# The down stage of a hybrid decoder step: prompt tokens stationary and 512 weight columns moving, the 32 sample tokens in full precision on four column groups

## The chip, the cores and the metric

The kernel runs on one core of a Trainium2 chip. Its engines are TensorE (PE; PEld in the profile is its weight load), VectorE (DVE), ScalarE (ACT), GpSimd (POOL) and SyncE (SP), which issues most DMAs. The metric is the device time of one execution in microseconds (us); lower is better.

## What is computed

One inference step of a two-layer decoder for 256 prompt tokens and 32 sample tokens (8 sequences of 4), model width 1024. The change touches the second half of the PEER channel mixer that ends each layer. There every one of 16384 experts has a row in `u_tab` and a row in `v_tab`; each token picks some experts, and

```python
act = jax.nn.gelu(jnp.einsum('td,thkd->thk', tb, u_tab[eb]))     # up
return jnp.einsum('thk,thkd->td', (gb * act), v_tab[eb])         # down
...
xp = xp + mp[5][:, None, :] * peer_ffn(...)                      # gated residual
```

The kernel computes it densely: a table W of 128 blocks x 128 experts holds for every token the gated activation (zero where the token did not pick the expert), and the down stage is the product y = W^T v over all 16384 experts: [288 tokens x 16384] times [16384 x 1024], in float32.

## The kernel before, in words

All weights come as 680 tiles of 128 x 1024 float32 words (512 KB) that SP loads in order into `ring`, a ring of four buffers; a buffer is loaded again when the PE has finished with its tile (semaphore `tile_done`). Float32 is reached with fp32r matmuls, in which each operand is split into a high part (an fp32r copy) and a low part (the rest): high x high, low x high and high x low, three passes. `wt_hi` (two buffers) is the high part of a weight tile, written by ACT (`high`, line 368, signals `hi_ready`); `ring_lo` lies on the same memory as `ring` and is the low part, written over the tile by DVE in this stage (line 2027, signals `lo_v`).

In the down stage of a layer (lines 1432 to 1456, 128 tiles for each of the two layers) tile j holds the rows of the 128 experts of block j. One tile is called a slot here. The activations `W[:, j]` (128 x 288) are split too: `w_hi` (two buffers, ACT, line 477, `wh_ready`) and `w_lo` (POOL, line 2116, `wl_ready`). For each of eight 128-column chunks c of the weight tile, the chunk is the stationary operand and the 288 tokens are the moving one; the sum of chunk c grows in PSUM bank c, with model columns on the partitions and tokens along the row. That makes 3 passes x 8 = 24 matmuls a slot (lines 1440, 1444, 1448). ACT prepares two tiles ahead: `down_high` waits for `tile_done` of slot n, then writes `w_hi` and `wt_hi` for tile n+2.

After the last slot DVE adds the sums to the residual stream `xT` with the gate (`residual`, lines 1748 to 1753, chunk by chunk out of PSUM), and the next part starts on its signal `x_ready`.

Two other places of the kernel matter for reading its trace. The V projection of the attention (lines 872 to 892) already has prompt tokens stationary and 512 weight columns moving in fp32r (`v_tile`, 884 and 892), and its 32 sample tokens in full precision on four column groups (`v_samples`, 872: four matmuls with 32 stationary columns each, whose results go to four groups of 32 partitions). The QK stage has a norm on four column groups (line 831, 288 columns) between two fp32r tiles (823 before it, 816 behind it).

Of the kernel before, what the change touches and what calls it, by code (L numbers as in the profile page):

```python
# [22 lines left out]
NC = D // P  # L23
SP_, SB, ST = 256, 8, 4
T = SP_ + SB * ST
# [22 lines left out]
UT, VT = (120, 424), (248, 552)  # L48
# [4 lines left out]
HI = (16, 52 + 256)  # L53
# [11 lines left out]
ACT = mybir.ActivationFunctionType  # L65
# [26 lines left out]
def build(nc, I, O):  # L92
    ctx = ExitStack()
    with ctx:
        def sb(name, words, dt=F32):
            return ctx.enter_context(nc.sbuf_tensor(name, [P, words], dt))

        def sem(name):
            return ctx.enter_context(nc.semaphore(name))


        big = sb("big", 128 * T)
# [16 lines left out]
        y_lo, y_hi = (split_t[:, z * NC * T:(z + 1) * NC * T].rearrange("p (c t) -> p c t", c=NC) for z in range(2))  # L119
        h_hi, h_lo = (split_t[:, z * NC * T:(z + 1) * NC * T].rearrange("p (c t) -> p c t", c=NC) for z in range(2))  # L120
        w_hi = w_hi_t[:, 0:2 * T].rearrange("p (b t) -> p b t", b=2)
        w_lo = split_t[:, 0:2 * T].rearrange("p (b t) -> p b t", b=2)
        xT_t = sb("xT", NC * T)
        xT = xT_t[:, :].rearrange("p (c t) -> p c t", c=NC)
# [2 lines left out]
        ada = ada_t[:, :].rearrange("p (l j c r) -> p l j c r", l=L, j=6, c=NC)  # L127
# [3 lines left out]
        ident = consts[:, 256:384]  # L131
# [10 lines left out]
        gtmp = sb("gtmp", 2 * T)  # L142
# [6 lines left out]
        ps = ctx.enter_context(nc.psum_tensor("ps", [P, 8, 512], F32))  # L149
# [14 lines left out]
        W = big[:, :].rearrange("p (j t) -> p j t", j=128)  # L164
# [103 lines left out]
        assert rb.at <= 128 * T - NC * T  # L268
        v_turn = gtmp[:, 0:512]
        jsum = small[:, 0:32]  # L270

        def unit_p(u):
            return (p_two if u >= H else p_one)[u % 4][:, 0:384 * (u // H + 1)]
# [31 lines left out]
        def kv_slot(n):  # L305
# [11 lines left out]
            "gelu_done w_done aq_copied aq_sq aq_ms aq_sd aq_qn aq_rot aq_done v_copied qz_ready "  # L317
            "us_mm us_half us_max us_exp us_t us_cpa us_cpv us_pv us_o ss_mm ss_max ss_exp ss_t ss_cp "
            "ss_norm ss_pv oT_ready out_done st_out kv_out glu_used_v "
            "aq_rc aq_sp hq_ready hq_lo hq_lo_v yh_ready yl_ready ss_oc ss_ot s5_rmr s5_zl hi_ready lo_u lo_v hh_ready hl_ready wh_ready wl_ready").split()}  # L320
        tile_in = [sem(f"tile_in{s}") for s in range(RING)]

        def tile_wait(eng, n, i=0):
# [41 lines left out]
        def high(act, n, i=0):  # L365

            tile_wait(act, n, i)
            nc.scalar.activation(wt_hi[:, n % 2], ring[:, n % RING], ACT.Copy).then_inc(S["hi_ready"], 1)  # L368

        def peer_act(act, l):  # L370
# [95 lines left out]
            for n in range(GROUPS):  # L466
                gate_high(n)
                if n == GROUPS - 1:
                    act.wait_ge(S["x_out"], 16 * (l + 1))
                    act.dma_start(xT_t[:, :], x_keep).then_inc(S["x_back"], 16)  # L470
                    for b in range(2):
                        nc.scalar.activation(w_hi[:, b], W[:, b], ACT.Copy).then_inc(S["wh_ready"], 1)
                gelu_split(n)


            def w_high(j, b):
                nc.scalar.activation(w_hi[:, b], W[:, bass.ds(j, 1), :].rearrange("p a t -> p (a t)"), ACT.Copy)\  # L477
                   .then_inc(S["wh_ready"], 1)

# [2 lines left out]
            def down_high(i, s):  # L482
                act.wait_ge(S["tile_done"], 4 * i + (VT[l] + s + 1))
                w_high(4 * i + (s + 2), s % 2)
                high(act, VT[l] + s + 2, i)
# [3 lines left out]
                    down_high(i, s)  # L489
            for s in range(2):  # L490
                down_high(31, s)

        def attention_act(act, root_mean):

# [589 lines left out]
        def _(pe):  # L1084
            mm = nc.tensor.matmul
# [214 lines left out]
            def peer_pe(l):  # L1300
# [87 lines left out]
                for n in range(2):  # L1388
                    for q in range(3):
                        ins = nc.tensor.transpose(ps[:, n, 128 * q:128 * q + 128],  # L1390
                                                  sel3[:, q, 8 * n:8 * n + 8, :].rearrange("p u k -> p (u k)"), ident)
                    ins.then_inc(S["sel_t"], 1)
                for q in range(3):
                    ins = mm(ps[:, 2, 32 * q:32 * q + 32], selz[:, q, :], jsel, start=True, stop=True)
# [35 lines left out]

                pe.wait_ge(S["gb_cp"], GROUPS * (l + 1))

                def down(i, first, last=False):
                    for s in range(4):
                        pe.wait_ge(S["hi_ready"], 4 * i + (HI[l] + 128 + s + 1))
                        pe.wait_ge(S["wh_ready"], 4 * i + (128 * l + s + 1))
                        for c in range(NC):
                            if first and s == 0 and c == 6:
                                pe.wait_ge(S["gelu_done"], 128 * (l + 1))
                            mm(ps[:, c, 0:T], wt_hi[:, s % 2, c * 128:(c + 1) * 128], w_hi[:, s % 2],  # L1440
                               start=(first and s == 0), stop=False, skip_group_check=True)
                        pe.wait_ge(S["wl_ready"], 4 * i + (128 * l + s + 1))
                        for c in range(NC):
                            mm(ps[:, c, 0:T], wt_hi[:, s % 2, c * 128:(c + 1) * 128], w_lo[:, s % 2],  # L1444
                               start=False, stop=False, skip_group_check=True)
                        pe.wait_ge(S["lo_v"], 4 * i + (LOV[l] + GROUPS + s + 1))
                        for c in range(NC):
                            ins = mm(ps[:, c, 0:T], ring_lo[:, s, c * 128:(c + 1) * 128], w_hi[:, s % 2],  # L1448
                                     start=False, stop=(last and s == 3), skip_group_check=True)
                        ins.then_inc(S["tile_done"], 1)  # L1450

                down(0, True)
                with pe.Fori(1, 31) as i:
                    down(i, False)
                down(31, False, True)

            peer_pe(0)
            mean_square(2)
# [119 lines left out]
        def _(v):  # L1578
            own = Count(v, S["v_own"])
            TT, TS, STT, CP = (nc.vector.tensor_tensor, nc.vector.tensor_scalar, nc.vector.scalar_tensor_tensor,  # L1580
                               nc.vector.tensor_copy)
# [8 lines left out]
            for r in range(4):  # L1590
                ins = nc.vector.memset(tmask[32 * r:32 * r + 32, 32 * r:128], 1.0)
# [97 lines left out]
            for z in range(2):  # L1689
# [183 lines left out]
            def peer_dve(l):  # L1873
                last = S["q_copied"]
                v.wait_ge(last, 8 * l + 8)
                TT(qsq, qraw, qraw, ALU.mult).then_inc(S["qsq_ready"], 1)
                for n in range(2):
# [4 lines left out]
                    ins = TT(q, q, r, ALU.mult)  # L1882
# [141 lines left out]
                with v.Fori(0, 32) as i:  # L2024
                    for s in range(4):
                        v.wait_ge(S["hi_ready"], 4 * i + (HI[l] + 128 + s + 1))
                        TT(ring_lo[:, s], ring[:, s], wt_hi[:, s % 2].bitcast(F32), ALU.subtract)\  # L2027
                            .then_inc(S["lo_v"], 1)
                v.wait_ge(S["x_back"], 16 * (l + 1))
                v.wait_ge(S["tile_done"], VT[l] + 128)  # L2030
                residual(ada[:, l, 5], ps[:, :, 0:T], 0, NC, gtmp[:, 0:256].rearrange("p (c t) -> p c t", c=NC),
                         S["x_ready"])

            modulate(1)
            ada_finish(1, 0, 6, 12)
# [261 lines left out]
```

## Time and profile before

| | |
|---|---|
| time of the kernel, median of 3 runs | 2474.07 us (2470.76 to 2480.36) |
| time of the profiled execution | 2485.71 us |
| its span, first to last instruction | 2483.9 us |
| busy: PE, DVE, ACT, POOL | 95%, 60%, 39%, 28% of the span |
| mean granted TensorE clock | 0.963 of full |
| down stage, layer 0 and layer 1 | 803.6 to 1212.3 us and 2066.7 to 2475.3 us |

The profile is one execution. Times in the rows are us from the span's start; a row of the timeline gives start, length, engine, line, operation, output<-inputs, shape and count, and in brackets the idle time before it with what ended it. A matmul that runs in full float32 shows as two records, one in fp32r as one. The two down stages together take a third of the span.

### The profile page before, as it was taken

Reading aid. Unit: us, or ns where it says so; the run is one execution under the profiler, and the core shown is the slowest. Engines: PE = TensorE matmul, PEld = TensorE weight load, DVE = VectorE, ACT = ScalarE, POOL = GpSimd, SP = SyncE. Lnnn points to the kernel's source line nnn. Section 1 sums busy time; section 2 is a strip of 40 time slices with the busy share of each in tenths; the row PEclk is TensorE's granted clock in tenths of the full one; section 3 lists DMA queues with packets and bytes.
Section 4 is the critical chain, followed back from the end, with each engine's and each line's share of the span. In section 5 each row is a group of like instructions: output and inputs, shape, how many; then the busy total and the mean of one; then the engine's idle time right before and its main releaser. Section 6 shows DMA issues by size and latency. Waiting matters only on the chain.

```text
span 2483.9 us, 50343 instructions
## 1 busy us (share of the span) xinstructions
PE 2361.9 (95%) x18518; PEld 2225.1 (90%) x18518; DVE 1478.9 (60%) x3301; ACT 979.5 (39%) x1675; POOL 705.1 (28%) x488
## 2 busy tenths in 40 slices
PE   6899999999999999999698977999999999999998
PEld 3578799999999999999697655999999999999998
DVE  8743369888898333333535442399688995333333
ACT  3234154444443444444332430443444434444443
POOL 2036267900000222222264200479300001222222
PEclk9968999999999999999899988999999999999999
DMA  8854544433334444444632662444433334444444
GB/s 311 286 181 159 203 138 165 138 136 128 127 127 144 163 165 164 166 163 168 241 127 94 257 252 98 136 161 142 143 128 129 127 127 165 167 163 166 165 165 137
DMA packets 105472, 404.98 MB, mean 163 GB/s; under 512 B 13377, under 2 KB 13633, under 8 KB 102177
## 3 DMA queue, kind: packets, MB, share of 16 engines
q1 hardware_dynamic: 99216, 360.84, 42.8%
q10 hardware_dynamic: 6160, 42.91, 4.4%
q8 instruction: 55, 0.90, 0.2%
q14 instruction: 41, 0.33, 0.0%
HBM read 394.56 MB, written 9.14 MB: 163 GB/s over the span
## 4 chain that ended last, share of the span: by engine, by line
PE 71%; issue 16%; POOL 9%; DMA 2%; DVE 2%; ACT 0%; ACTq 0%; SPq 0%; POOLq 0%; DVEq 0%
PE ps L1448 11%; PE ps L1440 11%; PE ps L1444 11%; POOL ring_lo L2098 8%; PE ps L1420 6%; PE ps L1419 6%; PE ps L1423 6%; PE ps L1407 5%; DMA ring<-in_stream 2%; PE ps L1094 2%; PE ps L1318 1%; POOL ring_lo L2105 1%; PE ps L816 1%; PE ps L820 1%; PE ps L823 1%
## 5 line engine op out<-in xcount | busy, mean ns | idle before, releaser
L368 ACT ACTIVATE wt_hi<-ring 128x1024 fp32r<-128x1024 f32 x564 | 593.9, 1053 | 344.6 <-PE ps L1318 209.5
L2027 DVE TENSOR_TENSOR ring_lo<-ring,wt_hi 128x1024 fp32r<-128x1024 f32 x256 | 314.7, 1230 | 492.1 <-ACT wt_hi L368 492.1
L2116 POOL TENSOR_TENSOR split<-big,w_hi 128x288 fp32r<-128x288 f32 x256 | 208.0, 813 | 1201.7 <-PE ps L1423 603.3
L2098 POOL TENSOR_TENSOR ring_lo<-ring,wt_hi 128x1024 fp32r<-128x1024 f32 x112 | 308.4, 2760 | 127.8 <-ACT wt_hi L368 127.8
L1419 PE MATMUL ps<-split,wt_hi 128*128 128x288 f32 x1152 | 328.5, 307 | 0.0
L1420 PE MATMUL ps<-split,wt_hi 128*128 128x288 f32 x1152 | 316.1, 298 | 0.0
L1448 PE MATMUL ps<-w_hi,ring_lo 128*128 128x288 f32 x2048 | 313.1, 295 | 1.4 <-DVE ring_lo L2027 1.4
L1444 PE MATMUL ps<-split,wt_hi 128*128 128x288 f32 x2048 | 313.1, 295 | 0.3
L1440 PE MATMUL ps<-w_hi,wt_hi 128*128 128x288 f32 x2048 | 312.9, 295 | 0.0
L477 ACT ACTIVATE w_hi<-big 128x288 fp32r (+1 forms) x252 | 112.0, 445 | 452.7 <-PE ps L1448 452.7
L1448 PEld LDWEIGHTS ps<-w_hi,ring_lo 128*128 128x128 f32 x2048 | 285.5, 188 | 1.9 <-DVE ring_lo L2027 1.9
L1444 PEld LDWEIGHTS ps<-split,wt_hi 128*128 128x128 f32 x2048 | 285.5, 188 | 0.8 <-POOL split L2116 0.8
L1440 PEld LDWEIGHTS ps<-w_hi,wt_hi 128*128 128x128 f32 x2048 | 285.5, 188 | 0.0
L1314 PE MATMUL ps<-split,wt_hi 128*128 128x288 f32 x896 | 247.4, 300 | 0.0
L1315 PE MATMUL ps<-split,wt_hi 128*128 128x288 f32 x896 | 244.7, 298 | 0.0
L1419 PEld LDWEIGHTS ps<-split,wt_hi 128*128 128x128 f32 x1152 | 217.6, 189 | 0.0
L1420 PEld LDWEIGHTS ps<-split,wt_hi 128*128 128x128 f32 x1152 | 217.3, 189 | 0.0
L1993 DVE TENSOR_SCALAR xT<-consts,idx 128x128 f32<-128x128 f32 x576 | 198.6, 345 | 0.0
L1992 DVE TENSOR_SCALAR xT<-consts,idx 128x128 f32<-128x128 f32 x576 | 165.1, 287 | 28.5 <-ACT idx L442 28.5
L1983 DVE TENSOR_TENSOR ring_lo<-ring,wt_hi 128x1024 fp32r<-128x1024 f32 x144 | 175.8, 1221 | 2.0 <-ACT wt_hi L368 0.8
L1423 PE MATMUL ps<-split,ring_lo 128*128 128x288 f32 x1152 | 176.9, 296 | 0.0
L460 ACT ACTIVATE gtmp<-ps 128x4 f32<-128x4 f32 (+23 forms) x144 | 42.2, 293 | 338.4 <-PE ps L1423 338.4
(336 smaller groups left out, 3463.0 us busy)
## 6 DMA issues: line engine op xcount, KB each, us to landing
ring<-in_stream SPq DMA_DIRECT2D x680, 512.0 KB, 3.3
big<-in_kc ACTq DMA_DIRECT2D x8, 1792.0 KB, 12.9
big<-in_vc ACTq DMA_DIRECT2D x8, 1792.0 KB, 9.9
out_qk<-big ACTq DMA_DIRECT2D x1, 3456.0 KB, 16.6
x_keep<-xT ACTq DMA_DIRECT2D x2, 1152.0 KB, 4.6
xT<-x_keep ACTq DMA_DIRECT2D x2, 1152.0 KB, 5.9
out_v<-big ACTq DMA_DIRECT2D x1, 1536.0 KB, 18.5
xT<-in_xT SPq DMA_DIRECT2D x1, 1152.0 KB, 9.8
```

The lines of the kernel that those rows point to most:

```text
L368: nc.scalar.activation(wt_hi[:, n % 2], ring[:, n % RING], ACT.Copy).then_inc(S["hi_ready"], 1)
L1314: mm(out, w, h_hi[:, c], start=(c == 0), stop=False)
L1315: mm(out, w, h_lo[:, c], start=False, stop=False)
L1419: mm(out, w, h_hi[:, c], start=(c == 0), stop=False)
L1420: mm(out, w, h_lo[:, c], start=False, stop=False)
L1423: ins = mm(out, ring_lo[:, s, c * 128:(c + 1) * 128], h_hi[:, c], start=False, stop=(c == NC - 1))
L1440: mm(ps[:, c, 0:T], wt_hi[:, s % 2, c * 128:(c + 1) * 128], w_hi[:, s % 2], start=(first and s == 0), stop=False, skip_group_check=True)
L1444: mm(ps[:, c, 0:T], wt_hi[:, s % 2, c * 128:(c + 1) * 128], w_lo[:, s % 2], start=False, stop=False, skip_group_check=True)
L1448: ins = mm(ps[:, c, 0:T], ring_lo[:, s, c * 128:(c + 1) * 128], w_hi[:, s % 2], start=False, stop=(last and s == 3), skip_group_check=True)
L2027: TT(ring_lo[:, s], ring[:, s], wt_hi[:, s % 2].bitcast(F32), ALU.subtract)\
L2098: TT(ring_lo[:, s], ring[:, s], wt_hi[:, s % 2].bitcast(F32), ALU.subtract)\
L2116: TT(w_lo[:, s % 2], W[:, bass.ds(4 * i + s, 1), :].rearrange("p a t -> p (a t)"), w_hi[:, s % 2].bitcast(F32), ALU.subtract).then_inc(S[" ...
```

## The change

- The 256 prompt tokens become the stationary operand, as two blocks of 128 (a), and the weight tile the moving one, as two halves of 512 columns (f). A pass is now 4 matmuls over 512 columns; three passes are 12 matmuls a slot. The sums of the prompt tokens stand in banks 0 to 3, with tokens on the partitions.
- The 32 sample tokens leave the three passes. ACT copies their activations to `w_new` (128 x 32, plain float32), and `new_tokens` multiplies them with the original float32 tile in `ring`: four matmuls with 32 stationary and 256 moving columns, one for each column group, all in bank 4. `new_tokens` of tile n+1 stands in slot n between the second and the third pass.
- Since `ring_lo` overwrites `ring`, DVE's low part of a tile now waits for `wn_used`, the end of `new_tokens` of that tile.
- At the end the sums have tokens on the partitions. ACT and DVE copy them from PSUM to `big`; PE turns them with 24 matmuls against the identity (for each of the eight chunks two of 128 columns and one of 32); DVE runs `residual` in two pieces, chunks 0 to 2 and 3 to 7. The wait for the last `gelu_done` moves from the first slot to this end.

```diff
+        w_new = idx_t[:, 2 * T:2 * T + 64].rearrange("p (b t) -> p b t", b=2)
+        y_tok = big[:, 0:2048].rearrange("p (a n) -> p a n", a=2)
+        y_new = big[:, 2048:2304]
...
             def w_high(j, b):
+                nc.scalar.activation(w_new[:, b], W[:, bass.ds(j, 1), 256:T].rearrange("p a t -> p (a t)"), ACT.Copy)
                 nc.scalar.activation(w_hi[:, b], W[:, bass.ds(j, 1), :].rearrange("p a t -> p (a t)"), ACT.Copy)\
                    .then_inc(S["wh_ready"], 1)
...
+            act.wait_ge(S["tile_done"], VT[l] + 128)
+            for b in range(2):
+                nc.scalar.activation(y_tok[:, 0, 512 * b:512 * b + 512], ps[:, b, :], ACT.Copy).then_inc(S["yo_a"], 1)
+            nc.scalar.activation(y_new, ps[:, 4, 0:256], ACT.Copy).then_inc(S["yo_a"], 1)
...
+                def new_tokens(n, s, begin, end):
+
+                    pe.wait_ge(S["hi_ready"], n + (HI[l] + 128 + 1))
+                    pe.wait_ge(S["wh_ready"], n + (128 * l + 1))
+                    for g in range(4):
+                        ins = mm(ps[32 * g:32 * g + 32, 4, 0:256], w_new[:, s % 2], ring[:, s % 4, 256 * g:256 * g + 256],
+                                 start=begin, stop=end, skip_group_check=True)
+                    ins.then_inc(S["wn_used"], 1)
+
                 def down(i, first, last=False):
                     for s in range(4):
...
                         pe.wait_ge(S["wh_ready"], 4 * i + (128 * l + s + 1))
-                        for c in range(NC):
-                            if first and s == 0 and c == 6:
-                                pe.wait_ge(S["gelu_done"], 128 * (l + 1))
-                            mm(ps[:, c, 0:T], wt_hi[:, s % 2, c * 128:(c + 1) * 128], w_hi[:, s % 2],
-                               start=(first and s == 0), stop=False, skip_group_check=True)
+                        for a in range(2):
+                            for f in range(2):
+                                mm(ps[:, 2 * a + f, :], w_hi[:, e, 128 * a:128 * a + 128], hi[f],
+                                   start=begin, stop=False, skip_group_check=True)
                         pe.wait_ge(S["wl_ready"], 4 * i + (128 * l + s + 1))
...
+                        if not end:
+                            new_tokens(4 * i + s + 1, s + 1, False, last and s == 2)
                         pe.wait_ge(S["lo_v"], 4 * i + (LOV[l] + GROUPS + s + 1))
-                        for c in range(NC):
-                            ins = mm(ps[:, c, 0:T], ring_lo[:, s, c * 128:(c + 1) * 128], w_hi[:, s % 2],
-                                     start=False, stop=(last and s == 3), skip_group_check=True)
+                        for a in range(2):
+                            for f in range(2):
+                                ins = mm(ps[:, 2 * a + f, :], w_hi[:, e, 128 * a:128 * a + 128], lo[f],
+                                         start=False, stop=end, skip_group_check=True)
                         ins.then_inc(S["tile_done"], 1)
...
+                pe.wait_ge(S["gelu_done"], 128 * (l + 1))
+                for c in range(NC):
+                    b = (c + 5) % 8
+                    if c % 4 == 0:
+                        pe.wait_ge(S["yo_a"], 3 * l + 1 + c // 4)
+                        pe.wait_ge(S["yo_v"], 2 * l + 1 + c // 4)
+                    for a in range(2):
+                        mm(ps[:, b, 128 * a:128 * a + 128], y_tok[:, a, 128 * c:128 * c + 128], ident, start=True, stop=True)
+                    if c == 0:
+                        pe.wait_ge(S["yo_a"], 3 * l + 3)
+                    mm(ps[:, b, 256:T], y_new[:, 128 * (c % 2):128 * (c % 2) + 128], ident[:, 32 * (c // 2):32 * (c // 2) + 32],
+                       start=True, stop=True)\
+                        .then_inc(S["yo_t"], 1)
...
                         v.wait_ge(S["hi_ready"], 4 * i + (HI[l] + 128 + s + 1))
+                        v.wait_ge(S["wn_used"], 4 * i + (128 * l + s + 1))
                         TT(ring_lo[:, s], ring[:, s], wt_hi[:, s % 2].bitcast(F32), ALU.subtract)\
                             .then_inc(S["lo_v"], 1)
...
-                residual(ada[:, l, 5], ps[:, :, 0:T], 0, NC, gtmp[:, 0:256].rearrange("p (c t) -> p c t", c=NC),
-                         S["x_ready"])
+                for f in range(2):
+                    CP(y_tok[:, 1, 512 * f:512 * f + 512], ps[:, 2 + f, :]).then_inc(S["yo_v"], 1)
+                for m0, m1 in ((0, 3), (3, 8)):
+                    v.wait_ge(S["yo_t"], 8 * l + m1)
+                    residual(ada[:, l, 5], ps[:, (m0 + 5) % 8:(m0 + 5) % 8 + m1 - m0, 0:T], m0, m1,
+                             gtmp[:, 32 * m0:32 * m1].rearrange("p (c t) -> p c t", c=m1 - m0),
+                             S["x_ready" if m0 else "x_some"])
```

Three places of the program in order. On the PE, one slot of the loop before (w_lo is the tile `split` here):

```order
L1436 REGISTER_ALU [waits hi_ready]
L1440 MATMUL ps<-w_hi,wt_hi 128x288 [waits wh_ready]
L1440 MATMUL ps<-w_hi,wt_hi 128x288 x7
L1444 MATMUL ps<-split,wt_hi 128x288 [waits wl_ready]
L1444 MATMUL ps<-split,wt_hi 128x288 x7
L1446 REGISTER_ALU
L1448 MATMUL ps<-w_hi,ring_lo 128x288 [waits lo_v]
L1448 MATMUL ps<-w_hi,ring_lo 128x288 x7
```

and the same slot of the change, where `idx` is the memory of `w_new`:

```order
L1458 REGISTER_ALU [waits hi_ready]
L1461 MATMUL ps<-wt_hi,w_hi 128x512 [waits wh_ready]
L1461 MATMUL ps<-wt_hi,w_hi 128x512 x3
L1466 MATMUL ps<-wt_hi,split 128x512 [waits wl_ready]
L1466 MATMUL ps<-wt_hi,split 128x512 x3
L1444 REGISTER_ALU
L1445 REGISTER_ALU [waits hi_ready]
L1447 MATMUL ps<-ring,idx 32x256 [waits wh_ready]
L1447 MATMUL ps<-ring,idx 32x256 x3
L1470 REGISTER_ALU
L1473 MATMUL ps<-ring_lo,w_hi 128x512 [waits lo_v]
L1473 MATMUL ps<-ring_lo,w_hi 128x512 x3
```

The wait for `hi_ready` of the next tile, which stood at the head of the next slot, now also stands ahead of the third pass of this one. On ACT, one slot before, up to the next slot's first row:

```order
L477 ISA [waits tile_done]
L477 ACTIVATE w_hi<-big 128x288
L368 ACTIVATE wt_hi<-ring 128x1024 [waits tile_in3]
L483 REGISTER_ALU
L477 ISA [waits tile_done]
```

and in the change:

```order
L481 ISA [waits tile_done]
L481 ACTIVATE idx<-big 128x32
L482 ISA
L482 ACTIVATE w_hi<-big 128x288
L371 ACTIVATE wt_hi<-ring 128x1024 [waits tile_in3]
L488 REGISTER_ALU
```

The copy to `w_new` stands between the wait for the PE and the two copies that the PE waits for. On DVE, the end of the stage in layer 0 before:

```order
L2024 COMPARE_AND_BRANCH
L1748 TENSOR_TENSOR gtmp<-ps,ada 128x256 [waits tile_done,x_back]
L1750 SCALAR_TENSOR_TENSOR xT<-ps,ada,xT 128x256 x8
L1753 TENSOR_TENSOR xT<-xT,gtmp 128x8x32 [waits v_own]
L1596 TENSOR_TENSOR big<-xT 128x1152 [waits x_ready]
```

and in the change:

```order
L2072 COPY big<-ps 128x512 [waits tile_done,x_back]
L2072 COPY big<-ps 128x512
L1787 TENSOR_TENSOR gtmp<-ps,ada 128x96 [waits yo_t]
L1789 SCALAR_TENSOR_TENSOR xT<-ps,ada,xT 128x256 x3
L1792 TENSOR_TENSOR xT<-xT,gtmp 128x3x32 [waits v_own]
L1787 TENSOR_TENSOR gtmp<-ps,ada 128x160 [waits yo_t]
L1789 SCALAR_TENSOR_TENSOR xT<-ps,ada,xT 128x256 x5
L1792 TENSOR_TENSOR xT<-xT,gtmp 128x5x32 [waits v_own]
L1635 TENSOR_TENSOR big<-xT 128x1152 [waits x_ready]
```

Between the last matmul of the stage and the residual stand now the copies and, on the PE, the turning that signals `yo_t`.

## Rows read from the trace of the kernel before

**Rows 1.** Windows: length, busy time of each engine, granted clock, DMA share, GB/s.

```profile
808.20:1211.90 403.70, 403.70 (x3049) 403.70 (x3048) 154.41 (x126) 175.80 (x252) 102.44 (x126) 1.00 0.49 165
1260.00:1345.00 85.00, 82.52 (x564) 74.89 (x563) 41.38 (x29) 26.79 (x42) 49.51 (x26) 1.00 0.36 118
1358.50:1414.00 55.50, 52.41 (x463) 34.31 (x462) 23.64 (x30) 18.61 (x24) 16.02 (x5) 1.00 0.53 197
```

**Rows 2.** Timeline of one slot in the middle of the stage, PE, ACT and DVE.

```profile
900.33 0.29 PE L1448 MATMUL ps<-w_hi,ring_lo 128*128 128x288 f32 x1
...
900.46 1.22 PE L1440 MATMUL ps<-w_hi,wt_hi 128*128 128x288 f32 x8
900.76 0.44 ACT L477 ACTIVATE w_hi<-big 128x288 fp32r x1 [1.79 <-PE ps L1448]
901.11 1.05 ACT L368 ACTIVATE wt_hi<-ring 128x1024 fp32r<-128x1024 f32 x1
902.19 1.23 DVE L2027 TENSOR_TENSOR ring_lo<-ring,wt_hi 128x1024 fp32r<-128x1024 f32 x1 [1.97 <-ACT wt_hi L368]
903.63 1.23 PE L1440 MATMUL ps<-w_hi,wt_hi 128*128 128x288 f32 x8
```

**Rows 3.** Timeline of the first slot, and the start of the last one.

```profile
803.65 1.22 PE L1440 MATMUL ps<-w_hi,wt_hi 128*128 128x288 f32 x8
805.20 2.96 DVE L2027 TENSOR_TENSOR ring_lo<-ring,wt_hi 128x1024 fp32r<-128x1024 f32 x2
807.08 1.32 PE L1448 MATMUL ps<-w_hi,ring_lo 128*128 128x288 f32 x8 [0.72 <-DVE ring_lo L2027]
808.24 0.56 PE L1440 MATMUL ps<-w_hi,wt_hi 128*128 128x288 f32 x3
...
1208.91 0.30 PE L1440 MATMUL ps<-w_hi,wt_hi 128*128 128x288 f32 x1
```

**Rows 4.** Timeline of PE in the V projection.

```profile
1384.06 1.08 PE L892 MATMUL ps<-ring_lo,split 128*128 128x512 f32 x4
1384.98 0.40 PE L884 MATMUL ps<-wt_hi,split 128*128 128x512 f32 x1
...
1387.55 0.40 PE L892 MATMUL ps<-ring_lo,split 128*128 128x512 f32 x1
1387.87 1.06 PE L872 MATMUL ps<-ring,big 128*32 128x512 f32 x8
1388.87 0.50 PE L884 MATMUL ps<-wt_hi,split 128*128 128x512 f32 x1
...
1389.21 0.39 PE L884 MATMUL ps<-wt_hi,split 128*128 128x512 f32 x1
```

**Rows 5.** Timeline of PE around one norm of the QK stage.

```profile
1279.29 0.29 PE L823 MATMUL ps<-split,ring_lo 128*128 128x288 f32 x1
...
1279.52 0.69 PE L831 MATMUL ps<-big,consts 128*32 128x288 f32 x8
...
1280.37 0.42 PE L816 MATMUL ps<-split,wt_hi 128*128 128x288 f32 x2
```

**Rows 6.** Timeline of ACT, two small operations from SBUF to SBUF.

```profile
17.42 0.23 ACT L657 ACTIVATE big<-big 128x32 f32<-128x32 f32 x1 [7.00 <-DVE big L1610]
17.55 0.21 ACT L658 ACTIVATE big<-big 128x32 f32<-128x32 f32 x1
```

**Rows 7.** Timeline of the end of the stage in layer 0.

```profile
1211.70 0.55 PE L1448 MATMUL ps<-w_hi,ring_lo 128*128 128x288 f32 x3
...
1212.70 3.22 DVE L1750 SCALAR_TENSOR_TENSOR xT<-ps,ada,xT 128x256 f32<-128x256 f32 x8
...
1216.42 2.63 DVE L1596 TENSOR_TENSOR big<-xT 128x1152 f32<-128x1152 f32 x2
```

**Rows 8.** Groups by line: shapes, count, busy us, mean ns, idle before.

```profile
L679 ACT ACTIVATE big<-ps 128x512 f32<-128x512 f32 x16 | 8.5, 601 | 15.5 <-PE ps L1152 15.3
```

**Rows 9.** Timeline of PE: four full-precision matmuls of 128 columns, 128 stationary.

```profile
510.65 1.05 PE L1407 MATMUL ps<-xT 128*128 128x128 f32 x8
```

More of the change, by code:

```diff
@@ L319, in build @@
             "ss_norm ss_pv oT_ready out_done st_out kv_out glu_used_v "
-            "aq_rc aq_sp hq_ready hq_lo hq_lo_v yh_ready yl_ready ss_oc ss_ot s5_rmr s5_zl hi_ready lo_u lo_v hh_ready hl_ready wh_ready wl_ready").split()}
+            "aq_rc aq_sp hq_ready hq_lo hq_lo_v yh_ready yl_ready ss_oc ss_ot s5_rmr s5_zl hi_ready lo_u lo_v hh_ready hl_ready wh_ready wl_ready wn_used yo_a yo_v yo_t x_some").split()}
         tile_in = [sem(f"tile_in{s}") for s in range(RING)]
@@ L471, in peer_act @@
                     for b in range(2):
+                        nc.scalar.activation(w_new[:, b], W[:, b, 256:T], ACT.Copy)
                         nc.scalar.activation(w_hi[:, b], W[:, b], ACT.Copy).then_inc(S["wh_ready"], 1)
@@ L1433, in down @@
                 def down(i, first, last=False):
                     for s in range(4):
+                        e = s % 2
+                        begin, end = first and s == 0, last and s == 3
+                        hi = [wt_hi[:, e, 512 * f:512 * f + 512] for f in range(2)]
+                        lo = [ring_lo[:, s, 512 * f:512 * f + 512] for f in range(2)]
                         pe.wait_ge(S["hi_ready"], 4 * i + (HI[l] + 128 + s + 1))
                         pe.wait_ge(S["wh_ready"], 4 * i + (128 * l + s + 1))
-                        for c in range(NC):
-                            if first and s == 0 and c == 6:
-                                pe.wait_ge(S["gelu_done"], 128 * (l + 1))
-                            mm(ps[:, c, 0:T], wt_hi[:, s % 2, c * 128:(c + 1) * 128], w_hi[:, s % 2],
-                               start=(first and s == 0), stop=False, skip_group_check=True)
@@ L1442, in down @@
-                        pe.wait_ge(S["wl_ready"], 4 * i + (128 * l + s + 1))
-                        for c in range(NC):
-                            mm(ps[:, c, 0:T], wt_hi[:, s % 2, c * 128:(c + 1) * 128], w_lo[:, s % 2],
-                               start=False, stop=False, skip_group_check=True)
+                        for a in range(2):
+                            for f in range(2):
+                                mm(ps[:, 2 * a + f, :], w_hi[:, e, 128 * a:128 * a + 128], hi[f],
+                                   start=begin, stop=False, skip_group_check=True)
@@ L1446, in down @@
+                        pe.wait_ge(S["wl_ready"], 4 * i + (128 * l + s + 1))
+                        for a in range(2):
+                            for f in range(2):
+                                mm(ps[:, 2 * a + f, :], w_lo[:, e, 128 * a:128 * a + 128], hi[f],
+                                   start=False, stop=False, skip_group_check=True)
+                        if not end:
+                            new_tokens(4 * i + s + 1, s + 1, False, last and s == 2)
                         pe.wait_ge(S["lo_v"], 4 * i + (LOV[l] + GROUPS + s + 1))
-                        for c in range(NC):
-                            ins = mm(ps[:, c, 0:T], ring_lo[:, s, c * 128:(c + 1) * 128], w_hi[:, s % 2],
-                                     start=False, stop=(last and s == 3), skip_group_check=True)
+                        for a in range(2):
+                            for f in range(2):
+                                ins = mm(ps[:, 2 * a + f, :], w_hi[:, e, 128 * a:128 * a + 128], lo[f],
+                                         start=False, stop=end, skip_group_check=True)
@@ L1450, in down @@
                         ins.then_inc(S["tile_done"], 1)
+                new_tokens(0, 0, True, False)
                 down(0, True)
@@ L1455, in peer_pe @@
                 down(31, False, True)
+                pe.wait_ge(S["gelu_done"], 128 * (l + 1))
[4 more added lines that the diff above has]
+                        pe.wait_ge(S["yo_v"], 2 * l + 1 + c // 4)
+                    for a in range(2):
+                        mm(ps[:, b, 128 * a:128 * a + 128], y_tok[:, a, 128 * c:128 * c + 128], ident, start=True, stop=True)
[4 more added lines that the diff above has]
+                        .then_inc(S["yo_t"], 1)
             peer_pe(0)
@@ L2030, in peer_dve @@
                 v.wait_ge(S["tile_done"], VT[l] + 128)
-                residual(ada[:, l, 5], ps[:, :, 0:T], 0, NC, gtmp[:, 0:256].rearrange("p (c t) -> p c t", c=NC),
-                         S["x_ready"])
+                for f in range(2):
+                    CP(y_tok[:, 1, 512 * f:512 * f + 512], ps[:, 2 + f, :]).then_inc(S["yo_v"], 1)
[4 more added lines that the diff above has]
+                             S["x_ready" if m0 else "x_some"])
             modulate(1)
```

## The prediction

> **What bounds the kernel now.** I read the windows first: in 403.70 us of the down stage the PE is busy for all 403.70, at a granted clock of 1.00, its upper level (2.4 GHz) [rows 1]. So the stage is bound by the PE's own stream. DVE, ACT and POOL are busy for 154, 176 and 102 us of it: they have room. The timeline then gives the size of a slot. Slots start at 808.24 and, 126 slots later, at 1208.91 [rows 3], which is 3.180 us a slot, or 0.1325 us for each of 24 matmuls of 288 columns. In the middle of the stage one sees the chain that feeds them [rows 2]: the last matmul of a slot starts at 900.33, ACT answers at 900.76 with `w_hi`, at 901.11 with `wt_hi`, and DVE gets that signal at 902.19, 1.86 us after the 900.33. The PE does not need it before the next slot at 903.63, so this chain is hidden by 1.4 us. The first slot is an exception: 4.59 us (803.65 to 808.24), because DVE's low part comes late [rows 3].
>
> **The full-width matmuls.** Twelve matmuls of 512 columns replace 24 of 288. The V projection has this very form: four of them start between 1384.06 and 1384.98 [rows 4], 0.230 us each (I take 0.231). Twelve cost 2.77 us, 0.41 less than 3.18. Stretching 0.1325 us by 512/288 would give 0.236, or 2.83 us, the upper bound. The stationary block of w_hi is loaded twice in a row; V loads a block for each matmul too, so its price is inside the 0.231.
>
> The Trainium skill (TensorE: Matmul & The Clock Gate, section Part 1) gives start to start of N / 2.4 GHz plus about 2.5 ns, so 0.216 us for 512 columns. That would make twelve 2.59 us. The row's 0.230 decides.
>
> **The block of new tokens.** Two places, both at a granted clock of 1.00 [rows 1], show what four column groups in full precision cost between full-width matmuls. The QK norm with 288 columns: last full-width start 1279.29, second full-width start behind the block 1280.37 [rows 5], 1.08 us, less two ordinary steps of 0.1325: 0.815 us. The V projection with 512 columns: 1387.55 to 1389.21 [rows 4], 1.66 us, less two steps of 0.231: 1.20 us. The difference, 0.385 us for 224 columns, is 0.0017 us a column; 256 columns cost 0.44 us, and 0.32 us is left whatever the size: the changeover into narrow groups (0.09 us, seen as 0.32 instead of 0.23 from 1387.55 to 1387.87) and out of them (0.34 us from 1388.87 to 1389.21 instead of 0.23, and the rest before it). The block costs 0.76 us. Below, with a changeover for nothing, it is 0.44.
>
> The Trainium skill (TensorEngine Tiling (Array Packing), section Key Properties) says that changing the tiling mode drains the engine, without a price; both rows agree, with 0.32 us.
>
> So the PE alone needs 2.77 + 0.76 = 3.53 us a slot in place of 3.18.
>
> **The loop of waits.** `new_tokens` of tile n+2 stands in slot n+1 ahead of the third pass and waits for `hi_ready` of n+2, which ACT can only give after `tile_done` of n. Before, this signal came 1.86 us after the last matmul's start. Now the matmul is longer (0.40 against 0.29 [rows 2, 4], +0.11) and the copy to `w_new` comes first: two ACT operations of 128x32 start 0.13 us apart [rows 6]. That makes 2.10 us; with 0.03 us (DVE's answer to 902.16) to 0.1 us until the PE moves, the block may start at 2.13 to 2.20. The PE arrives there after nine steps of 0.231 and 0.09 of changeover: 2.17. The two meet, and the cover of 1.4 us is gone. The loop adds 0 to 0.05 us; I take 3.55 us a slot (3.50 to 3.65). What counts is that the loop holds even where the PE prices are too high: 2.15, then 0.44 for the block, then 0.69 to the last start of the third pass is 3.28.
>
> **What lies beside it.** DVE's low part now starts after `wn_used`, some 2.8 us into slot n-1, and takes 1.23 us; it ends about 0.5 us into slot n, and the third pass wants it at 2.8: free, with over 2 us of cover. Behind DVE's wait stands only the next low part. POOL's w_lo comes 0.14 us later and has a slot to spare. SP's loads follow `tile_done` as before, with one issue a slot at a lower rate. DMA was busy for 0.49 [rows 1]. ACT's 0.23 us more per slot has room except on the loop.
>
> **Start and end of the stage.** The first slot keeps its length: the third pass waits for DVE until 807.08 [rows 3], and `new_tokens` of tiles 0 and 1 fit in front of it. The last slot has no block. The end grows. Before: last matmul over at 1212.25, next part starts at 1216.42 [rows 7], 4.17 us. Now: an ACT copy of 128x512 from PSUM (0.60 us [rows 8]) and DVE's beside it, then the PE can turn the first blocks at 0.8 us; the third ACT copy ends near 1.6 us; 24 turns are 48 records of at most 0.13 us (eight take 1.05 with the last one's full length [rows 9], at least 0.11), so 5.3 to 6.3 us, ending about 7.5 us after the last matmul; of the residual the last five chunks remain, 4.17 less three steps of 0.39 (3.22 for eight [rows 7]), so 3.0. That is 10.5 instead of 4.2: +6.3 us a layer, 13 us in all. If the clock fell to its lower level during the turns, up to 6 us more a layer.
>
> **Sum.** 252 slots x (3.55 - 3.18 = 0.37) = +93 us, ends +13, first and last slots -1: +105 us. The profiled execution at 2485.71 becomes 2591. The median of the runs is 11.6 us lower (2474.07); with the same difference the median becomes **2579 us**, +4.2%.
>
> **Rivals.**
> *The loop binds harder* (signal late, by register work around `w_new` on ACT, or groups started one by one after a wait). The two register rows on ACT speak for it; against it, ACT's register work already stands beside running copies. A slot of 3.75: 254 x 0.57 + 13 = 158, 2632 us.
> *The changeover is free*: the block costs 0.44 and the loop then sets 3.28 us: 254 x 0.10 + 13 = 38, 2512 us. Against it: both rows of the trace, 0.32 us each.
> *Faster*: the narrow groups run beside full-width matmuls and cost nothing of their own. Then after 2.15 us only 0.69 us of third pass follows, 2.84 us a slot: -86 + 13 = -73, 2401 us. It decides the sign when a slot is below 3.13 (13 us of ends over 254 slots). Against it: in the V projection no full-width matmul starts between 1387.55 and 1388.87 [rows 4].
>
> By the Trainium skill's step of 0.216 us (the page named first) and a block of 0.44 without changeover, the PE would need 3.03 us a slot, and the time would be 2474 - 38 + 13 = 2449 us, faster; the loop of waits would still hold the slot above 3.2.
>
> **Numbers.** Forecast (slot 3.50 to 3.65, 2555 to 2610): 0.77. Loop harder (2610 to 2660): 0.10. Cheaper changeover (2500 to 2555): 0.08. Faster: 0.03, the page's case included. Near no change: 0.02. A measurement of this kernel can tell about 0.5% from no change. Range 2535 to 2622. Slower 0.95, within 0.5% 0.02, faster 0.03.
>
> **What would show it.** Right: 512-column matmuls 0.23 us apart; 0.32 us into the block, 0.56 across it (1.00 from 1387.87 to 1388.87 [rows 4], less 0.44 for 256 columns fewer) and 0.34 for the first step behind it; a slot of 3.55; little or no idle PE ahead of `new_tokens`; the granted clock at 1.00; 10 us from the last matmul to the next part. Wrong: steps of 0.216; third-pass matmuls that start within the block; idle time in front of `new_tokens` with ACT's `wt_hi` as its releaser of more than 0.1 us a slot; a slot under 3.2; a granted clock that falls inside the stage, which would make the time far longer than the range.

## The result and the profile after

The changed kernel took 2596.18 us in the median of 4 runs (2590.20 to 2607.09), the kernel before 2472.55 us: a ratio of 1.0493 (95% interval 1.0449 to 1.0537), slower, as forecast, 17 us above the predicted 2579 and inside the range (2535 to 2622). Six more runs beside eleven of the kernel before gave 2585.0 against 2474.26 us, a ratio of 1.0446 (1.0417 to 1.0475). The profiled execution took 2591.18 us, 105.5 us more than that of before.

The windows of the changed kernel over its two down stages (columns as in [rows 1]):

```profile
803.50:1256.00 452.50, 451.52 (x2520) 295.95 (x2519) 153.72 (x127) 190.78 (x378) 102.23 (x126) 1.00 0.44 146
2124.00:2572.00 448.00, 448.00 (x2519) 293.96 (x2518) 153.51 (x127) 190.84 (x378) 102.06 (x126) 1.00 0.43 145
```

The PE is as busy as before and its granted clock is again 1.00: nothing was lost to the clock in these stages, they hold more PE time. The weight loads (second count) shrank from all of the window to two thirds of it, and yet the slots grew.

The timeline of one slot in layer 0, which answers to [rows 2]:

```profile
911.39 1.10 PE L1461 MATMUL ps<-wt_hi,w_hi 128*128 128x512 f32 x4
911.79 0.23 ACT L481 ACTIVATE idx<-big 128x32 f32 x1 [2.14 <-PE ps L1473]
...
912.26 1.04 ACT L371 ACTIVATE wt_hi<-ring 128x1024 fp32r<-128x1024 f32 x1
912.33 1.09 PE L1466 MATMUL ps<-wt_hi,split 128*128 128x512 f32 x4
913.03 0.39 PE L1466 MATMUL ps<-wt_hi,split 128*128 128x512 f32 x1
913.43 0.64 PE L1447 MATMUL ps<-ring,idx 128*32 128x256 f32 x8
914.00 1.20 PE L1473 MATMUL ps<-ring_lo,w_hi 128*128 128x512 f32 x4
914.33 0.39 PE L1473 MATMUL ps<-ring_lo,w_hi 128*128 128x512 f32 x1
915.03 1.08 PE L1461 MATMUL ps<-wt_hi,w_hi 128*128 128x512 f32 x4
```

Read it from 912.26: the high part of the next tile ends at 913.30, the block of new tokens starts at 913.43. The last full-width matmul had started at 913.03, so the step into the block is 0.40 us where 0.32 is the step with a changeover and no wait: this block waits for ScalarE. The block then takes 0.57 us to the next full-width start (914.00), and the first step behind it 0.33. Full-width matmuls start 0.233 us apart here (three steps from 912.33 to 913.03), against 0.230 in [rows 4].

Starts of the slots 1 and 127 of the changed kernel, layer 0 and layer 1 (timeline, the first matmul of a slot):

```profile
803.48 0.39 PE L1461 MATMUL ps<-wt_hi,w_hi 128*128 128x512 f32 x1
1256.45 0.39 PE L1461 MATMUL ps<-wt_hi,w_hi 128*128 128x512 f32 x1
2124.01 0.39 PE L1461 MATMUL ps<-wt_hi,w_hi 128*128 128x512 f32 x1
2572.67 0.39 PE L1461 MATMUL ps<-wt_hi,w_hi 128*128 128x512 f32 x1
```

That is 452.97 us for 126 slots, 3.595 us each, in layer 0, and 448.66, 3.561, in layer 1, against 3.180 in both layers before [rows 3]. The two layers run the same code in two different patterns; the part on the prediction comes back to that.

The end of the stage in layer 0, which answers to [rows 7]:

```profile
1258.53 0.86 PE L1473 MATMUL ps<-ring_lo,w_hi 128*128 128x512 f32 x3
...
1259.50 1.29 DVE L2072 COPY big<-ps 128x512 f32<-128x512 f32 x2 [2.72 <-PE ps L1473]
...
1260.33 0.68 PE L1489 MATMUL ps<-consts,big 128*128 128x128 f32 x4 [0.94 <-DVE big L2072]
...
1265.63 0.31 PE L1492 MATMUL ps<-consts,big 128*128 128x32 f32 x2
1265.98 0.32 DVE L1787 TENSOR_TENSOR gtmp<-ps,ada 128x160 f32<-128x160 f32 x1 [1.63 <-PE ps L1492]
...
1268.65 1.36 DVE L1635 TENSOR_TENSOR big<-xT 128x1152 f32<-128x1152 f32 x1
```

From the last matmul's end (1259.39) to the next part (1268.65) pass 9.26 us, 0.94 of them until the first turn, 5.6 for the turning and 2.7 for the last five chunks; before it was 4.17.

### The profile page after: what moved, and what is told of

Its sections match the earlier page's. It is cut to its first block, busy times and chain, and to the rows that moved or that the text cites. A ratio compares the mean times of both kernels' runs of the same rounds, so it can differ in the third digit from the quotient of the medians.

```text
span 2589.4 us, 49581 instructions
## 1 busy us (share of the span) xinstructions
PE 2469.7 (95%) x17590; PEld 2021.3 (78%) x17590; DVE 1481.3 (57%) x3309; ACT 1012.2 (39%) x1937; POOL 704.4 (27%) x488
## 4 chain that ended last, share of the span: by engine, by line
PE 71%; issue 15%; POOL 9%; DVE 2%; DMA 2%; ACT 0%; SPq 0%; POOLq 0%; ACTq 0%; DVEq 0%
PE ps L1473 11%; PE ps L1461 9%; PE ps L1466 9%; POOL ring_lo L2143 7%; PE ps L1429 6%; PE ps L1428 6%; PE ps L1432 6%; PE ps L1447 6%; PE ps L1416 5%; DMA ring<-in_stream 2%; PE ps L1103 1%; PE ps L1327 1%; POOL ring_lo L2150 1%; PE ps L825 1%; PE ps L829 1%
## 5 line engine op out<-in xcount | busy, mean ns | idle before, releaser
L1428 PE MATMUL ps<-split,wt_hi 128*128 128x288 f32 x1152 | 328.5, 307 | 0.0
L1429 PE MATMUL ps<-split,wt_hi 128*128 128x288 f32 x1152 | 316.1, 298 | 0.0
L1473 PE MATMUL ps<-ring_lo,w_hi 128*128 128x512 f32 x1024 | 306.0, 420 | 0.2
L1461 PE MATMUL ps<-wt_hi,w_hi 128*128 128x512 f32 x1024 | 279.5, 395 | 0.0
L1466 PE MATMUL ps<-wt_hi,split 128*128 128x512 f32 x1024 | 278.2, 393 | 0.0
L1473 PEld LDWEIGHTS ps<-ring_lo,w_hi 128*128 128x128 f32 x1024 | 172.5, 188 | 127.8 <-issue 103.8
L481 ACT ACTIVATE idx<-big 128x32 f32 (+1 forms) x252 | 57.9, 230 | 522.2 <-PE ps L1473 522.2
L1323 PE MATMUL ps<-split,wt_hi 128*128 128x288 f32 x896 | 246.8, 300 | 0.0
L1324 PE MATMUL ps<-split,wt_hi 128*128 128x288 f32 x896 | 244.1, 298 | 0.0
L1461 PEld LDWEIGHTS ps<-wt_hi,w_hi 128*128 128x128 f32 x1024 | 192.2, 188 | 45.9 <-issue 0.8
L1466 PEld LDWEIGHTS ps<-wt_hi,split 128*128 128x128 f32 x1024 | 192.8, 188 | 45.1
L1428 PEld LDWEIGHTS ps<-split,wt_hi 128*128 128x128 f32 x1152 | 217.6, 189 | 0.0
L1429 PEld LDWEIGHTS ps<-split,wt_hi 128*128 128x128 f32 x1152 | 217.3, 189 | 0.0
L2032 DVE TENSOR_SCALAR xT<-consts,idx 128x128 f32<-128x128 f32 x576 | 195.6, 340 | 0.0
L2031 DVE TENSOR_SCALAR xT<-consts,idx 128x128 f32<-128x128 f32 x576 | 162.7, 282 | 28.4 <-ACT idx L445 28.4
```

The source lines that it names most:

```text
L1323: mm(out, w, h_hi[:, c], start=(c == 0), stop=False)
L1324: mm(out, w, h_lo[:, c], start=False, stop=False)
L1428: mm(out, w, h_hi[:, c], start=(c == 0), stop=False)
L1429: mm(out, w, h_lo[:, c], start=False, stop=False)
L1461: mm(ps[:, 2 * a + f, :], w_hi[:, e, 128 * a:128 * a + 128], hi[f], start=begin, stop=False, skip_group_check=True)
L1466: mm(ps[:, 2 * a + f, :], w_lo[:, e, 128 * a:128 * a + 128], hi[f], start=False, stop=False, skip_group_check=True)
```

## The experiments

Times are medians against runs of the kernel before on the same chip; slots are (start of slot 127 - start of slot 1) / 126 of the profile in layer 0, where no layer is named.

**No block (e1_no_block).** The narrow blocks are taken out of the loop, all but the one of tile 0; the sums of the sample tokens are left out with them.

```diff
-                        if not end:
-                            new_tokens(4 * i + s + 1, s + 1, False, last and s == 2)
...
-                        v.wait_ge(S["wn_used"], 4 * i + (128 * l + s + 1))
+                        if l == 0:
+                            v.wait_ge(S["wn_used"], 1)
+                        else:
+                            v.wait_ge(S["wn_used"], 2)
```

> The change without the narrow blocks in the loop (only tile 0 keeps its block, so the sums of the 32 sample tokens are left out). Theory (twelve full-width matmuls at 0.231 us, and a block that costs all the rest of the slot): slots of 2.77 to 2.80 us in place of 3.56 to 3.60, 200 us below the changed kernel, about 3.4% below the kernel before. Rival (the chain through ScalarE, 2.2 us from the last matmul of a slot to its signal, binds without the block too): slots above 3.0 us. Second rival (full-width matmuls are slower in this stage than in the V projection): steps above 0.24 us.

2381.04 us, 94 below the kernel before, ratio 0.9602 (0.9539 to 0.9664). The timeline gives the slots 1 and 127:

```profile
808.68 0.39 PE L1461 MATMUL ps<-wt_hi,w_hi 128*128 128x512 f32 x1
...
1158.95 0.40 PE L1461 MATMUL ps<-wt_hi,w_hi 128*128 128x512 f32 x1
```

2.780 us a slot, 0.2317 us a matmul. Both rivals fall: the full-width matmuls cost here what they cost in the V projection, and without the block the chain through ScalarE does not bind. The gain is a little larger than expected (4.0% where I said 3.4%). The blocks account for all that the change loses, and more.

**A signal of its own (e2_own_signal).** `new_tokens` waits for its tile's landing and for the copy to `w_new`, not for the tile's high part.

```diff
-                    pe.wait_ge(S["hi_ready"], n + (HI[l] + 128 + 1))
-                    pe.wait_ge(S["wh_ready"], n + (128 * l + 1))
+                    tile_wait(pe, VT[l] + s, i)
+                    pe.wait_ge(S["wn_ready"], n + (128 * l + 1))
```

(and `.then_inc(S["wn_ready"], 1)` on the copies to `w_new`)

> The narrow block waits for the landing of its tile and for a signal of its own from the copy to w_new, and no longer for the high part of that tile. Loop theory: the step into the block falls from 0.344 us on average to 0.32 to 0.33, no two kinds of slots are left, all slots 3.53 to 3.55, 8 to 12 us below the changed kernel. Rival (the 0.344 is the changeover itself and the wait costs nothing): same time within 2 us.

2584.81 us, ratio 1.0436 (1.0345 to 1.0527): too wide to tell 10 us in the time. The profile tells it: starts at slots 1 and 127 of layer 0, then of layer 1.

```profile
810.57 0.39 PE L1462 MATMUL ps<-wt_hi,w_hi 128*128 128x512 f32 x1
1256.19 0.39 PE L1462 MATMUL ps<-wt_hi,w_hi 128*128 128x512 f32 x1
2121.24 0.39 PE L1462 MATMUL ps<-wt_hi,w_hi 128*128 128x512 f32 x1
2566.90 0.39 PE L1462 MATMUL ps<-wt_hi,w_hi 128*128 128x512 f32 x1
```

3.537 us in both layers: the two patterns are gone, 0.058 and 0.024 us a slot are won, 10 us in all. Over all blocks of the two traces the step into the block falls from 0.344 us on average (0.356 in layer 0, 0.332 in layer 1) to 0.322. So the loop of waits did bind, and 3.537 is the PE's own price. With the slot of 2.780 without blocks, a block costs 0.757 us (0.76 in the prediction).

**Half the columns (e3_half_columns).** As e2_own_signal, with 128 of 256 columns in each block but the first; half of the sample tokens' sums are left out.

```diff
+                        m = 256 if begin else 128
-                        ins = mm(ps[32 * g:32 * g + 32, 4, 0:256], w_new[:, s % 2], ring[:, s % 4, 256 * g:256 * g + 256],
+                        ins = mm(ps[32 * g:32 * g + 32, 4, 0:m], w_new[:, s % 2], ring[:, s % 4, 256 * g:256 * g + m],
```

> As e2_own_signal, with 128 of the 256 columns in every narrow block but the first (half of the sums of the sample tokens are left out). Theory (0.0017 us a column and 0.32 us for the changeover whatever the size): slots shorter by 0.22 us than in e2_own_signal, 55 us below it. Rival (all of the block's 0.77 us goes with its columns): shorter by 0.38 us, 97 us below it. Second rival (the block is all changeover): no difference.

2511.91 us, ratio 1.0160 (1.0089 to 1.0230), 73 us below the run with whole blocks; the slots (791.24 to 1209.97, 3.323 us) say 0.214 us a slot, 54 us. The two profiled executions also differ by 19 us ahead of the first down stage (slot 1 at 791.24 here and at 810.57 there), which this edit does not touch.

```profile
791.24 0.39 PE L1463 MATMUL ps<-wt_hi,w_hi 128*128 128x512 f32 x1
...
1209.97 0.39 PE L1463 MATMUL ps<-wt_hi,w_hi 128*128 128x512 f32 x1
```

0.214 us for 128 columns is 0.00167 us a column. Of the 0.757 us, 0.43 go with the 256 columns and 0.33 stay whatever the size.

**Blocks in pairs (e4_pairs).** As e2_own_signal, with four `w_new` buffers filled a slot earlier, and the blocks of two tiles together in every second slot.

```diff
-                        if not end:
-                            new_tokens(4 * i + s + 1, s + 1, False, last and s == 2, i)
+                        if s % 2 == 0:
+                            for d in (1, 2):
+                                if not (last and s + d > 3):
+                                    new_tokens(4 * i + s + d, s + d, False, last and s + d == 3, i)
```

> As e2_own_signal, with the narrow blocks of two tiles one behind the other in every second slot. Theory (0.32 us is paid for each change between narrow and full width, not for each tile): a pair of slots is shorter by 0.32 us than two of e2_own_signal, about 40 us below it, a mean slot of 3.37 us, still slower than the kernel before by about 60 us. Rival (the price is one of each tile, by its weight loads): same time as e2_own_signal.

2534.86 us, ratio 1.0257 (1.0179 to 1.0335), 50 us below e2_own_signal, of which the slots hold 41, as expected. Slots 1 to 127 and one pair:

```profile
791.87 0.39 PE L1464 MATMUL ps<-wt_hi,w_hi 128*128 128x512 f32 x1
...
1005.95 1.07 PE L1450 MATMUL ps<-ring,idx 128*32 128x256 f32 x16
1006.95 1.19 PE L1478 MATMUL ps<-ring_lo,w_hi 128*128 128x512 f32 x4
...
1216.92 0.39 PE L1464 MATMUL ps<-wt_hi,w_hi 128*128 128x512 f32 x1
```

3.373 us a mean slot, 0.164 less: half of 0.33. Two blocks of 8 records run from 1005.95 to 1006.95, 1.00 us, against 0.57 for one: the second costs 0.43, its columns. The price of 0.33 us is one of the changeover, not of the tile.

A changeover here is two changes at once: from full width to 32 stationary columns, and from fp32r to full precision. The kernel before shows the second one alone, in the up stage, where four full-precision matmuls with all 128 stationary columns and 128 moving ones (eight records) stand between fp32r matmuls of 288 columns, at a granted clock of 1.00:

```profile
509.59 1.23 PE L1423 MATMUL ps<-split,ring_lo 128*128 128x288 f32 x8
510.65 1.05 PE L1407 MATMUL ps<-xT 128*128 128x128 f32 x8
511.46 0.38 PE L1419 MATMUL ps<-split,wt_hi 128*128 128x288 f32 x1
511.68 0.30 PE L1420 MATMUL ps<-split,wt_hi 128*128 128x288 f32 x1
```

The step into them is an ordinary one (eight steps from 509.59 to 510.65, 0.1325 us each). From 510.65 to the second fp32r start behind, 511.68, pass 1.03 us; less one ordinary step that is 0.90 us for 512 moving columns, which at 0.00167 us a column are 0.855. So full precision by itself costs at most 0.04 us beyond its columns, and the 0.33 us belong to the narrow groups.

**The change once more (e5_change_again)**, unedited.

> The changed kernel once more, to tell its real distance from the kernel before: the two profiles differ by 105 us, the medians of the first runs by 123 us. Theory (the change costs what its stage and its ends show in the trace, 109 us, and the rest are other stages that vary from run to run): ratio 1.040 to 1.047, and the slots of the profile again between 3.55 and 3.60 us at a granted clock of 1.00. Rival (the stage itself is slower in some executions): ratio near 1.050, and a profile with slots above 3.60 us or a clock below 1.00 in the stage.

2585.0 us against 2474.26, 1.0446 (1.0417 to 1.0475): +110.7 us. Its profile has the slots of the first one:

```profile
788.55 0.39 PE L1461 MATMUL ps<-wt_hi,w_hi 128*128 128x512 f32 x1
1241.53 0.39 PE L1461 MATMUL ps<-wt_hi,w_hi 128*128 128x512 f32 x1
2109.13 0.39 PE L1461 MATMUL ps<-wt_hi,w_hi 128*128 128x512 f32 x1
2557.55 0.39 PE L1461 MATMUL ps<-wt_hi,w_hi 128*128 128x512 f32 x1
```

3.595 us in layer 0 and 3.559 in layer 1. The stage repeats to a few ns a slot, though this execution took 15 us less than the first profile: the work ahead of the first down stage (slot 1 at 788.55 instead of 803.48) holds those 15. In its first 200 us the granted clock was 0.78 in the first profile and 0.86 in this one. So of the first medians' 124 us the traces put 109 on the change, and the rest is of the size by which the work outside the changed stages varies.

**The small copy twice (e6_copy_twice).** The changed kernel, with a second copy of 128x32 on ScalarE in each slot.

```diff
             def w_high(j, b):
+                nc.scalar.activation(w_spare[:, b], W[:, bass.ds(j, 1), 256:T].rearrange("p a t -> p (a t)"), ACT.Copy)
                 nc.scalar.activation(w_new[:, b], W[:, bass.ds(j, 1), 256:T].rearrange("p a t -> p (a t)"), ACT.Copy)
```

> The changed kernel with the copy of 128x32 on ScalarE done twice in every slot (the second into unused words). Loop theory (the block waits for ScalarE's chain, with nothing left over): the chain is longer by 0.13 us, the mean slot grows from 3.58 to 3.69 to 3.73 us, 28 to 38 us above the changed kernel. Rival (TensorE sets the slot and the chain has cover): no change.

2607.61 us, ratio 1.0527 (1.0493 to 1.0561), 22.6 us above the changed kernel.

```profile
799.21 0.39 PE L1463 MATMUL ps<-wt_hi,w_hi 128*128 128x512 f32 x1
...
1002.46 0.23 ACT L482 ACTIVATE idx<-big 128x32 f32 x1 [2.05 <-PE ps L1475]
...
1003.05 1.04 ACT L372 ACTIVATE wt_hi<-ring 128x1024 fp32r<-128x1024 f32 x1
1004.22 0.64 PE L1449 MATMUL ps<-ring,idx 128*32 128x256 f32 x8
...
1264.09 0.39 PE L1463 MATMUL ps<-wt_hi,w_hi 128*128 128x512 f32 x1
...
2126.74 0.39 PE L1463 MATMUL ps<-wt_hi,w_hi 128*128 128x512 f32 x1
...
2589.48 0.39 PE L1463 MATMUL ps<-wt_hi,w_hi 128*128 128x512 f32 x1
```

3.690 us in layer 0 and 3.673 in layer 1: +0.095 and +0.11 us a slot, 26 us in all. The chain grew by 0.12 us, not 0.13: from the first small copy to the high part it takes 0.59 us (1002.46 to 1003.05), 0.47 in the changed kernel (911.79 to 912.26). The high part ends at 1004.09 and the block starts at 1004.22, 0.13 us behind its release, as in the changed kernel. There that holds for nearly every block, too: 121 of 127 in layer 0 and 90 in layer 1 start 0.13 us behind the end of the high part, whatever the step into them. So the loop set nearly every slot before the copy was doubled. The result is less than expected (22.6 us by the medians, where I said 28 to 38). In layer 1 the 0.01 us that are missing were free: about every fourth block (30 of 127) starts 0.137 us behind the high part, after a step of 0.317 us, as without a wait. In layer 0 a delay of ScalarE that the changed kernel has in every fourth slot (see What stays open) is absent here.

**The small copy twice, with a signal of its own (e7_copy_twice_own_signal).** The same line in e2_own_signal.

> The same second copy in e2_own_signal. Loop theory: the block no longer waits for the copies of the high parts, the chain has its old cover of over 1 us, slots stay at 3.537 us, same time as e2_own_signal. Rival (ScalarE's work costs the stage something in itself): slower by up to 30 us.

2571.42 us, ratio 1.0401 (1.0359 to 1.0443), 36 us below the same copy without the signal.

```profile
786.70 0.39 PE L1464 MATMUL ps<-wt_hi,w_hi 128*128 128x512 f32 x1
...
1003.37 1.05 ACT L372 ACTIVATE wt_hi<-ring 128x1024 fp32r<-128x1024 f32 x1
1004.42 0.64 PE L1450 MATMUL ps<-ring,idx 128*32 128x256 f32 x8
...
1232.36 0.39 PE L1464 MATMUL ps<-wt_hi,w_hi 128*128 128x512 f32 x1
```

3.537 us again. Here the block starts at 1004.42 while the high part is just ending (1003.37 + 1.05): it no longer follows it. ScalarE's work as such costs the stage nothing.

**The old form with the prompt tokens alone (e8_before_prompts_only).** The kernel before, with 256 moving tokens in place of 288 (the sums of the sample tokens are left out behind the first pass of the first tile).

```diff
-                            mm(ps[:, c, 0:T], wt_hi[:, s % 2, c * 128:(c + 1) * 128], w_lo[:, s % 2],
+                            mm(ps[:, c, 0:256], wt_hi[:, s % 2, c * 128:(c + 1) * 128], w_lo[:, s % 2, 0:256],
```

(and the same in the other two passes)

> The kernel before with 256 moving tokens in the down stage in place of 288 (the sums of the 32 sample tokens are left out behind the first pass of the first tile). It prices what the sample tokens cost while they ride along, and the old form for the prompt tokens alone. Theory (a matmul costs by its columns, 0.44 ns for each and some 6 ns, the line through 0.1325 us at 288 and 0.231 us at 512 columns): 0.118 us a matmul, slots of 2.84 us, about 87 us below the kernel before. So the sample tokens cost 0.35 us a slot there against 0.77 in the changed kernel, and the old form is within 0.06 us of the 2.78 us of e1_no_block. Rival (the weight load of 128 columns sets 0.1325 us): slots stay at 3.18 us, no change.

2392.05 us, ratio 0.9691 (0.9628 to 0.9754), 79 us below the kernel before.

```profile
794.49 0.28 PE L1441 MATMUL ps<-w_hi,wt_hi 128*128 128x256 f32 x1
...
1154.85 0.28 PE L1441 MATMUL ps<-w_hi,wt_hi 128*128 128x256 f32 x1
```

2.860 us a slot, 0.119 us a matmul. So 32 sample tokens that ride along as 32 of 288 moving columns cost 3.180 - 2.860 = 0.32 us a slot, and for the prompt tokens alone the new form (2.780) is only 0.08 us better than the old one. The rival, a floor set by the weight load, falls.

## Why the prediction was right

**Full-width matmuls**: 0.231 us said, 0.2317 measured (no block). The step of 0.216 that the Trainium skill gives (TensorE: Matmul & The Clock Gate, section Part 1) is not reached in any run here.

**The block**: 0.76 us said, 0.757 measured, split 0.43 and 0.33 (half the columns) where the prediction had 0.44 and 0.32. That the 0.33 is paid for each change of width is shown by the pairs.

**The loop of waits**: the prediction had it meet the PE's own stream and add 0 to 0.05 us, 3.55 us in all. It adds 0.024 in layer 1 and 0.058 in layer 0; the mean slot is 3.578. This is the term that was mis-sized, by 7 us. Layer 1 is the loop as predicted: on average 2.06 us from a slot's last matmul start to the end of the high part and 0.13 until the block starts, 2.19, where the PE was to arrive at 2.17. Most of the 7 us, 5.7, is layer 0, with two delays that the prediction did not have (see What stays open). The mechanism is shown from both sides: taking the wait off gives 3.537, lengthening the chain lengthens the slot, and the two together give 3.537 again. One mark could not tell right from wrong: idle PE in front of the block. The rows show next to none (451.52 of 452.50 us busy) although the loop binds, because the record of the full-width matmul ahead lasts 0.39 us and covers most of the wait; it is seen only in the step, 0.40 in place of 0.32.

**Start and end**: the ends were put at +6.3 us a layer and took +5.1 (9.26 against 4.17). The turning took 5.6 us, at the low side of its bounds, and was over 6.55 us after the last matmul, where 7.5 was said; the last five chunks took 2.7 instead of 3.0. The first slot did not keep its length: 4.38 us with its block (799.10 to 803.48) against 4.59.

**The sum**: 252 slots at +0.398 us are +100 us, the ends +10, the first and last slots -1: +109 us, where the sum said 93 + 13 - 1 = 105. (The stage from its first matmul to its last took 460.3 and 456.0 us instead of 408.6 each.) That 7 us too little in the loop and 3 too much at the ends partly cancel is luck. The medians of the longer run differ by 110.7.

**The rivals**: a free changeover and narrow groups beside full-width matmuls are both out by the block's 0.757 us. Of the loop that binds harder a small part came true, in layer 0; even the doubled copy, at 3.69 us, stays below its 3.75.

What the prediction did not say is where the gain of the 512 columns had gone: of the 0.41 us that it credited to twelve matmuls in place of 24, 0.32 was only the sample tokens that had left. The exchange is 0.32 us of riding along against 0.757 of blocks and 0.04 of waiting, for 0.08 gained on the prompt tokens. By these numbers no number of tiles per block would mend it: even with the changeover for nothing, 2.78 + 0.43 = 3.21 us (an estimate) is above 3.18. None of the versions run here beats the kernel before with all its outputs.

**What stays open**: why the loop settles in a pattern of 3.595 us in layer 0 and 3.56 in layer 1, in both profiles of the change. The trace shows where the difference lies, though not why. Four slots in a row of layer 0 (the copies to `w_new`, and one block):

```profile
904.53 0.23 ACT L481 ACTIVATE idx<-big 128x32 f32 x1 [2.05 <-PE ps L1473]
...
906.17 0.69 PE L1447 MATMUL ps<-ring,idx 128*32 128x256 f32 x8
906.79 0.50 PE L1473 MATMUL ps<-ring_lo,w_hi 128*128 128x512 f32 x1
...
908.13 0.23 ACT L481 ACTIVATE idx<-big 128x32 f32 x1 [2.09 <-PE ps L1473]
...
911.79 0.23 ACT L481 ACTIVATE idx<-big 128x32 f32 x1 [2.14 <-PE ps L1473]
...
915.35 0.23 ACT L481 ACTIVATE idx<-big 128x32 f32 x1 [2.04 <-PE ps L1473]
```

About one block in four (29 of 127) starts its second column group 0.05 us late, so that 0.62 us pass to the next full-width start (906.17 to 906.79) instead of 0.57. And in about every fourth slot the copy to `w_new` starts 0.63 us behind the last matmul's start instead of 0.55: hence the 3.66 us from 908.13 to 911.79. Together that is some 0.14 us in four slots, 0.035 each, which is all of the difference between the layers; layer 1 has neither delay. With the doubled copy layer 0 has only the late groups, and the layers differ by 0.017. In e2_own_signal layer 0 has the late copies and loses nothing by them, since its blocks do not wait for the high part. The loops of PE and ScalarE hold four slots a turn; why the delays come, and only in layer 0, no run here shows.

## What to carry to other kernels

Before a few rows are taken out of a wide matmul and given one of their own, price them where they are: as extra moving columns they cost their share of the stream, apart they cost a form with its own rate and its changeovers. The price of a changeover can be read wherever the kernel already makes one: from the start of the last matmul before to the second start behind it, less two ordinary steps and the block's own columns. And a wait moved forward in a loop is priced by the cover that it had: 1.4 us were used up here without a single new long operation.

## What the runs showed of the hardware that was not expected

The line through two sizes (0.1325 us at 288 columns, 0.231 at 512) held at a third: 0.119 us at 256, against 0.118 from the line. And the price of the changeover into narrow groups and back, 0.33 us by blocks of 128 and 256 columns, held for blocks of twice 256 (and was 0.32 by the blocks of 288 and 512 columns in [rows 4, 5]); full precision at full width had no such price (at most 0.04 us).
